# Sample values and sample outputs of a gated recurrence, carried through DRAM

## The chip, the cores and the metric

The kernel runs on one core of a Trainium2 chip. The metric is the device time of one execution in microseconds, the median of several runs. The engines are named as in the profile: PE (TensorE), DVE (VectorE), ACT (ScalarE), POOL (GpSimd), SP (SyncE, which here only issues DMAs).

## The reference

One inference step of two layers over 1024 prompt tokens and 8 sample tokens (one new token in each of 8 sequences), width 1024, all in fp32. The first layer is a gated linear recurrence (HGRN2) with 8 heads of 128 keys and 128 values, the second a sliding-window attention. The change touches only the first layer, and in it only the 8 sample tokens. For a head, cut to what matters:

```python
u = rmsnorm(h, norm_g) @ w_in
q, f, i, g = split(u)
q = silu(q);  k = (1 - lb) * sigmoid(-f);  v = i          # decay f_t = sigmoid(f) + lb * sigmoid(-f)
# prompt: chunkwise over 1024 tokens; sample: one step from the state s0 of each sequence b
S[b] = diag(decay[b]) @ s0[b] + outer(k[b], v[b])         # 128 keys x 128 values, an output
o[b] = S[b].T @ q[b]                                      # 128 values
o = rmsnorm(o, gnorm) * silu(g);  h = h + o @ w_out
```

So each head needs, for each of the 8 sequences b, an outer product of keys and values that is added to a decayed 128x128 state, and a product of that state with the query. In the program's layout the features lie on the partitions and the tokens along the row: a tile of T = 1032 columns holds 1024 prompt tokens and then the 8 sample tokens.

## The kernel before

**The loop.** The first layer's projection is a loop of HEADS + 1 = 9 turns `it`, each with 9 slots. In turn `it` the slots compute the projections of head `it` (three weight blocks of 128 columns, f, q and v; a block takes three `unit`s of 344 token columns, 24 matmuls each, L1569), while the recurrence of head r = it - 1 runs between the units on PE, and at slot 0 the output of head p = it - 2. Turn 8 has the first gate blocks in its units, and the sums for the heads' norms. The output of head 7 follows behind the loop (L1705), then two units, then its norm sums `head_sums(7)` (L1708).

**Slot 8 and slot 0.** At slot 8 PE does `value_broadcast(r)` (L1625) and `chunk_sums(r)` (L1631). The sample state keeps keys on partitions and (sequence, value) along the row, so the update needs each sequence's values on all 128 partitions. POOL's `decode_parts` (L649) multiplies the sample columns of RAWV with the identity into VD (128 x 1024) in slot 4; PE multiplies VD with a matrix of ones, which puts the values on every partition in two PSUM banks, VB0 and VB1; DVE's `decode_state` (L1142) multiplies these with the keys into VK, `decode_add` (L1151) adds VK to the decayed state SS, and `chunk_states` (L1157) makes the eight prompt states ST. DVE does these behind the evacuation of slot 8's unit. At slot 0 of the next turn PE does a unit, then `head_output` (L1640): 8 chunks, each with VH x AT (L1647) and, from the second on, ST x QU (L1650), which waits for its step of ST; then the sample outputs OS (L1655), 8 matmuls with SS of a sequence as the 128x128 stationary operand and one query column moving, which write 8 columns. Behind it comes `diagonal` of head r (L1596), 32 matmuls on four quarters of 32 columns of the array. It waits for `q1_done`, which DVE's `first_query` (L1109) signals; that waits for the group O1, the second half of the head output, as it overwrites QU.

**Banks.** The recurrence's PSUM groups (`turn_groups`, L54) take five banks in turn; a group waits until the one five before it is read. ACT's `copy_head` (L811) copies O0, O1 and OS into A, the sample columns of A from the 8 columns of OS. ACT's `square_head` (L817) squares all 1032 columns of A of a head for its norm sums.

**Queues.** Each engine runs its instructions in the written order and waits for semaphores. All DMAs are issued by SP (L451 on). In a turn SP issues three weight loads (each waits until POOL has made the low part of the block three before, `lo_value`), `states(it - 1)` (SS from DRAM, waits for the OS of the head before) and `store_states(it - 1)`. A weight load fills one of three buffers; its block is prepared by ACT (L751) once the block three before is done on PE. A matmul of the recurrence (plain fp32) is two instructions in the profile, one of the units (fp32r) is one.

Of the kernel before, what the change touches and what calls it, by code (L numbers as in the profile page):

```python
# [21 lines left out]
P = 128  # L22
KT = D // P
SEQ, DEC = 1024, 8
# [29 lines left out]
def turn_groups(it):  # L54

    slots = [[] for _ in range(9)]
    tail, rec = it - 2, it - 1
    if 0 <= tail < HEADS:
        slots[0] += [("O0", tail, "act"), ("O1", tail, "act"), ("OS", tail, "act")]
    if 0 <= rec < HEADS:  # L60
        slots[0] += [(f"D{i}", rec, "dve") for i in range(NC // 2)]
        for s in range(1, NL):
            slots[s].append((f"L{s}", rec, "dve"))
        slots[2] += [("VT0", rec, "act"), ("VT1", rec, "act")]
        slots[7] += [("T0", rec, "act"), ("T1", rec, "act")]
        slots[8] += [("VB0", rec, "prod"), ("VB1", rec, "prod"), ("S0", rec, "state"), ("S1", rec, "state")]
    if it == HEADS:
        for m in range(HEADS - 1):
            slots[m + 1] += [(f"N{i}", m, "act") for i in range(NU)]
    if it == HEADS + 1:  # L70
        slots[2] += [(f"N{i}", HEADS - 1, "act") for i in range(NU)]
    return [g for s in slots for g in s]
# [55 lines left out]
def build(nc, ctx, ins, outs):  # L128
# [3 lines left out]
    x_d, w_d, gain_d, lbl_d, st_d, lmask_d, imask_d, ident_d, cs_d, amask_d, smask_d, sink_d, sinks_d, kc_d, vc_d = ins  # L132
    y_d, stp_d, sts_d, kwin_d, vwin_d = outs
    h1_d = nc.dram_tensor("h1_spill", [P, KT, T], fp32, kind="Internal").ap()
    sg_d = nc.dram_tensor("gate_spill", [P, HP, T], fp32, kind="Internal").ap()


# [81 lines left out]
    PSN = sb("PSN", [DEC, P], fp32, rk)  # L219

    rp = [max(ra[0], rb_[0])]
    amask = sb("amask", [P, 2 * P], fp32, rp)
    sink = sb("sink", [P, 16], fp32, rp)
    smask = sb("smask", [P, DEC], fp32, rp)
# [15 lines left out]
    def sem(name):  # L240
        return ctx.enter_context(nc.semaphore(name))
# [29 lines left out]
    upd_k = sem("upd_k")  # L271
    fp_step = sem("fp_step")
    fp_done = sem("fp_done")
    vd_done = sem("vd_done")
    ss_in = sem("ss_in")
    ss_decayed = sem("ss_decayed")
    ss_prod = sem("ss_prod")
# [1 line left out]
    st_step = sem("st_step")  # L279
    stp_out = sem("stp_out")  # L280
    sts_out = sem("sts_out")
    sqn_done = sem("sqn_done")
    rn_done = sem("rn_done")
    norm_done = sem("norm_done")
# [96 lines left out]
    def half(i):  # L381
        return slice(i * 512, (i + 1) * 512)
# [4 lines left out]
    def read_value(r, name):  # L387
        who = GROUPS[GINDEX[name, r]][2]
        if who == "state":
            return st_step, NC * r + 4 * (int(name[1]) + 1)  # L390
        if who == "prod":
            return ss_prod, 2 * r + int(name[2]) + 1
        return (read_act if who == "act" else read_dve), READ_COUNT[name, r]

    def bank(r, name):
        return R[GINDEX[name, r] % NBANK_R]
# [55 lines left out]
    def _(sp):  # L452
# [32 lines left out]
        states(0)  # L485
        load_weights(3)
        load_weights(4)
        for it in range(HEADS + 1):
            load_weights(3 * it + 5)
            if it >= 2:  # L490
                states(it - 1)
            load_weights(3 * it + 6)
            load_weights(3 * it + 7)
            if it >= 1:
                store_states(it - 1)

        for n in range(N_AO, N_AO + 3):
            load_weights(n)

# [7 lines left out]
        first_residual(1)  # L507
        sp.wait_ge(stp_out, 16 * HEADS)
        sp.wait_ge(sts_out, 16 * HEADS)
        for t, d in ((amask, amask_d), (sink, sink_d), (smask, smask_d), (sinks, sinks_d), (CS, cs_d)):  # L510
            sp.dma_start(t[:], d).then_inc(const2_in, 16)
        for m in range(KT):
# [93 lines left out]
    def _(pool):  # L606
# [40 lines left out]
                                    ).then_inc(upd_k, 1)  # L647

        def decode_parts(r):  # L649
            pool.wait_ge(unit_read, 9 * r + 9)  # L650
            if r:
                pool.wait_ge(ss_prod, 2 * r)
            nc.gpsimd.tensor_tensor(VD[:, 0:SEQ].rearrange("p (b e) -> p b e", b=DEC),
                                    ident[:].unsqueeze(1).broadcast_to([P, DEC, P]),
                                    RAWV[:, SEQ:T].unsqueeze(2).broadcast_to([P, DEC, P]), ALU.mult).then_inc(vd_done, 1)
            pool.wait_ge(ss_in, 16 * (r + 1))
            pool.wait_ge(fp_done, r + 1)
            nc.gpsimd.tensor_tensor(SS[:], SS[:], DECC[:, r % 2, NC:].unsqueeze(2).broadcast_to([P, DEC, P]), ALU.mult
                                    ).then_inc(ss_decayed, 1)
# [82 lines left out]
    def _(act):  # L742
# [66 lines left out]
                nc.scalar.activation(dst[:, half(i)], bank(r, f"{name}{i}")[:], ACT.Copy).then_inc(read_act, 1)  # L809

        def copy_head(p):  # L811
            for name, cols in (("O0", half(0)), ("O1", half(1)), ("OS", slice(SEQ, T))):
                act.wait_ge(group_done, group_value(p, name))
                nc.scalar.activation(A[:, p, cols], bank(p, name)[:, 0:cols.stop - cols.start], ACT.Copy
                                     ).then_inc(read_act, 1)

        def square_head(m):  # L817
            if m == 0:
                act.wait_ge(ss_prod, 2 * (HEADS - 1))
            else:  # L820
                act.wait_ge(group_done, group_value(m - 1, "N2"))
            act.wait_ge(read_act, READ_COUNT["OS", m])
            nc.scalar.activation(SQN[:], A[:, m, :], ACT.Square).then_inc(sqn_done, 1)

        def norm_head(m):
# [240 lines left out]
    def _(dve):  # L1066
# [74 lines left out]

        def decode_state(r):  # L1142
            for i in range(2):
                dve.wait_ge(group_done, group_value(r, f"VB{i}"))
                dve.wait_ge(k_done, r + 1)
                nc.vector.tensor_tensor(VK[:, half(i)].rearrange("p (b e) -> p b e", b=4),
                                        bank(r, f"VB{i}")[:].rearrange("p (b e) -> p b e", b=4),
                                        K[r % 2][:, SEQ + 4 * i:SEQ + 4 * i + 4].unsqueeze(2).broadcast_to([P, 4, P]),
                                        ALU.mult).then_inc(ss_prod, 1)

# [61 lines left out]
        for it in range(HEADS + 1):  # L1212
            r = it - 1
            for slot in range(9):
                j, i = divmod(slot, 3)
                if slot == 0 and it:
                    dve.wait_ge(k_done, it)
                if slot == 3 and it:
                    dve.wait_ge(q_done, it)
                if slot == 6 and it:  # L1220
                    dve.wait_ge(group_done, group_value(it - 1, "VT1"))
                if slot == 8 and it:
                    dve.wait_ge(vd_done, it)
                evacuate(9 * it + slot, i, (RAWF, RAWQ, RAWV)[j])
                if r >= 0:
                    if slot == 0:
                        first_query(r)
                        for c in range(NC // 2):
                            merge_diagonal(r, c)
                    if 0 < slot < NL:  # L1230
                        update_q(r, slot)
                        merge_level(r, slot)
                    if slot == 8:
                        decode_state(r)
                        decode_add(r)
                        chunk_states(r)
                if slot == 7 and it < HEADS:
                    apply_query_gate(it)
                if it == HEADS and slot >= 2:
                    apply_norm(slot - 2)  # L1240
# [306 lines left out]
    def _(pe):  # L1547
# [74 lines left out]
                                           by_blocks(QU[:, first:first + w], l)[:, :, 1, :], start=True, stop=True)  # L1622
            ins.then_inc(group_done, 1)

        def value_broadcast(r):  # L1625
            pe.wait_ge(vd_done, r + 1)
            for i in range(2):
                b = open_group(r, f"VB{i}")
                nc.tensor.matmul(b[:], ones[:], VD[:, half(i)], start=True, stop=True).then_inc(group_done, 1)  # L1629

        def chunk_sums(r):  # L1631
            for i in range(2):
                pe.wait_ge(*read_value(r, f"T{i}"))
# [6 lines left out]
        def head_output(r):  # L1640
            pe.wait_ge(*read_value(r, f"L{NL - 1}"))
            pe.wait_ge(upd_q, NL * r + NL)
            for i in range(2):
                b = open_group(r, f"O{i}")
                for c in range(4 * i, 4 * i + 4):
                    cols = b[:, (c % 4) * P:(c % 4 + 1) * P]
                    ins = nc.tensor.matmul(cols, VH[:, c, :], AT[:, c, :], start=True, stop=(c == 0))  # L1647
                    if c:
                        pe.wait_ge(st_step, NC * r + c)
                        ins = nc.tensor.matmul(cols, ST[:, c - 1, :], QU[:, c * P:(c + 1) * P], start=False, stop=True)  # L1650
                ins.then_inc(group_done, 1)
            pe.wait_ge(ss_done, r + 1)
            b = open_group(r, "OS")
            for n in range(DEC):
                ins = nc.tensor.matmul(b[:, n:n + 1], SS[:, n, :], QDEC[:, r % 2, n:n + 1], start=True, stop=True)  # L1655
            ins.then_inc(group_done, 1)

        def head_sums(m):
# [20 lines left out]
        for it in range(HEADS + 1):  # L1679
            p, r = it - 2, it - 1  # L1680
            for slot in range(9):
# [4 lines left out]
                if r >= 0:  # L1686
# [10 lines left out]
                        for i in range(2):  # L1697
                            transposed(r, f"T{i}", K[r % 2], i)
                    if slot == 8:
                        value_broadcast(r)  # L1700
                        chunk_sums(r)
                if it == HEADS and 1 <= slot < HEADS:
                    head_sums(slot - 1)
# [253 lines left out]
```

## Time and profile before

| | |
|---|---|
| median of 3 runs | 1076.44 us (1076.37 to 1076.47) |
| the profiled execution | 1076.68 us, its span 1074.9 us |
| PE, DVE, POOL, ACT busy | 1033.7, 619.2, 436.0, 385.1 us |
| a steady turn of the loop (160.78 to 211.44) | 50.66 us |
| the last turn (414.15 to 477.08) | 62.93 us |

Line numbers are those of the kernel before. Busy times of PE overlap, as matmuls are pipelined: what an instruction costs is the distance between its start and that of the next one. In a timeline row the numbers are its start and its length in microseconds, x16 means that 16 instructions are merged, and what stands in brackets is the idle time of the engine before it and who ended it. PEld is the loading of the stationary operand.

### The profile page before, as it was taken

How to read it: one execution, taken by the hardware profiler on the slowest of the kernel's cores; microseconds unless marked ns; L12 is line 12 of the kernel's file. 1: busy time of each engine (PE TensorE's matmuls, PEld its weight loads, DVE VectorE, ACT ScalarE, POOL GpSimd, SP SyncE). 2: the span in 40 equal slices, each digit the busy share in tenths (PEclk: the TensorE clock that was granted, in tenths of full speed). 3: DMA queues.
4: the chain of work that ended last, by engine and by line, in shares of the span. 5: the costliest groups of instructions: out<-in, count | busy, mean ns of one | idle time of the engine just before them, and what ended most of it. 6: DMA issues, size and time to landing. Idle time of an engine off the chain costs nothing.

```text
span 1074.9 us, 22442 instructions
## 1 busy us (share of the span) xinstructions
PE 1033.7 (96%) x9392; PEld 964.5 (90%) x9392; DVE 619.2 (58%) x1195; ACT 385.1 (36%) x775; POOL 436.0 (41%) x294
## 2 busy tenths in 40 slices
PE   6999999999999999999999999999989999898996
PEld 5899999999999999899999999999988888677895
DVE  8153645554555546454843235357777878987835
ACT  4412212121213132645333233501037757654523
POOL 1245554645546463521225441343445333322243
PEclk9999999999999999999999999999989989999998
DMA  7111112021111202011314323211112113322103
GB/s 281 40 41 41 65 39 83 21 82 41 63 62 41 82 26 78 22 40 43 124 60 166 130 79 136 80 46 53 47 45 67 60 60 100 89 71 60 48 33 125
DMA packets 39812, 77.10 MB, mean 72 GB/s; under 512 B 5792, under 2 KB 24736, under 8 KB 39584
## 3 DMA queue, kind: packets, MB, share of 16 engines
q1 hardware_dynamic: 39712, 75.67, 21.2%
q8 instruction: 74, 1.21, 0.5%
q14 instruction: 26, 0.21, 0.1%
HBM read 58.12 MB, written 17.54 MB: 70 GB/s over the span
## 4 chain that ended last, share of the span: by engine, by line
PE 77%; DVE 12%; ACT 6%; issue 3%; POOL 1%; DMA 0%; DVEq 0%; SPq 0%; ACTq 0%; POOLq 0%
PE G L1566 54%; PE G L1821 4%; DVE SP L1403 4%; ACT SP L983 3%; PE R L1619 3%; DVE QNL L1388 3%; PE R L1669 1%; PE R L1593 1%; PE R L1636 1%; PE R L1647 1%; DVE PT L1421 1%; PE R L1629 1%; PE R L1655 1%; PE R L1662 1%; PE R L1650 1%
## 5 line engine op out<-in xcount | busy, mean ns | idle before, releaser
L1566 PE MATMUL G<-XH,WH 128*128 128x344 f32 x1176 | 387.3, 329 | 1.9 <-DVE RAWF L1079 1.9
L1566 PE MATMUL G<-XL,WH 128*128 128x344 f32 x1176 | 379.4, 323 | 2.3 <-DVE KE L1373 1.9
L1566 PE MATMUL G<-XH,WL 128*128 128x344 f32 x744 | 238.3, 320 | 0.0
L1566 PEld LDWEIGHTS G<-XH,WH 128*128 128x128 f32 x1176 | 223.0, 190 | 5.8 <-issue 2.2
L1566 PEld LDWEIGHTS G<-XL,WH 128*128 128x128 f32 x1176 | 222.9, 190 | 5.1 <-DVE WL L1069 2.2
L615 POOL TENSOR_TENSOR WL<-WR,WH 128x1024 fp32r<-128x1024 f32 x40 | 102.1, 2553 | 181.8 <-ACT WH L760 181.8
L760 ACT ACTIVATE WH<-WR 128x1024 fp32r<-128x1024 f32 x58 | 61.1, 1055 | 263.1 <-PE G L1566 167.1
L1566 PEld LDWEIGHTS G<-XH,WL 128*128 128x128 f32 x744 | 140.4, 189 | 0.0
L1566 PE MATMUL G<-XL,WL 128*128 128x344 f32 x432 | 139.7, 323 | 0.0
L646 POOL TENSOR_TENSOR K<-K,FP 128x512 f32<-128x512 f32 x48 | 77.6, 1617 | 90.5 <-PE R L1619 90.5
L698 POOL TENSOR_TENSOR SP<-SP,small 128x1024 f32<-128x1024 f32 (+1 forms) x32 | 57.3, 1790 | 136.0 <-DVE small L1414 136.0
L983 ACT ACTIVATE SP<-SP,small 128x256 f32<-128x256 f32 (+1 forms) x128 | 61.8, 484 | 68.4 <-DVE small L1403 68.4
L1566 PEld LDWEIGHTS G<-XL,WL 128*128 128x128 f32 x432 | 82.5, 191 | 0.4
L1079 DVE TENSOR_TENSOR RAWQ<-G,RB 128x344 f32<-128x344 f32 x27 | 14.0, 517 | 82.4 <-PE G L1566 82.4
L1566 PE MATMUL G<-GR,WL 128*128 128x344 f32 x192 | 61.4, 320 | 0.0
L1566 PE MATMUL G<-GR,WH 128*128 128x344 f32 x192 | 61.4, 320 | 0.0
L1566 PE MATMUL G<-AR,WH 128*128 128x344 f32 x192 | 61.3, 319 | 0.0
L1079 DVE TENSOR_TENSOR RAWV<-G,RB 128x344 f32<-128x344 f32 x27 | 14.0, 517 | 73.1 <-PE G L1566 73.1
L1403 DVE CUSTOM_DVE_ANT_0 SP<-R,amask,sink 128x256 f32<-128x256 f32 (+1 forms) x128 | 51.9, 458 | 1.5 <-PE R L1767 1.5
L1821 PE MATMUL G<-XL,WH 128*128 128x344 f32 x144 | 47.9, 333 | 0.5 <-DVE AR L1523 0.5
L714 POOL TENSOR_TENSOR KE<-KE,CS 128x1032 f32<-128x1032 f32 x8 | 27.2, 3395 | 49.5 <-DVE KE L1377 49.5
L1821 PE MATMUL G<-XL,WL 128*128 128x344 f32 x144 | 46.0, 319 | 0.0
(253 smaller groups left out, 1978.2 us busy)
## 6 DMA issues: line engine op xcount, KB each, us to landing
WR<-w SPq DMA_DIRECT2D x58, 512.0 KB, 3.6
A<-x SPq DMA_DIRECT2D x8, 516.0 KB, 8.3
RESO<-x SPq DMA_DIRECT2D x8, 516.0 KB, 4.7
h_spill<-H SPq DMA_DIRECT2D x8, 516.0 KB, 2.9
gate_spill<-EV SPq DMA_DIRECT2D x24, 172.0 KB, 1.9
RES<-h_spill SPq DMA_DIRECT2D x24, 172.0 KB, 3.0
y<-H SPq DMA_DIRECT2D x24, 172.0 KB, 1.9
SS<-states SPq DMA_DIRECT2D x8, 512.0 KB, 3.6
```

What stands on the lines that cost most here:

```text
L615: nc.gpsimd.tensor_tensor(WL[:, n % 3], WR[:, n % 3], WH[:, n % 3].bitcast(fp32), ALU.subtract).then_inc(lo_pool, 1)
L646: nc.gpsimd.tensor_tensor(low, low, decay(l, 1).unsqueeze(2).broadcast_to([P, SEQ // (2 * h), h]), ALU.mult).then_inc(upd_k, 1)
L698: nc.gpsimd.tensor_tensor(sp_, sp_, small[:, q % 2, 4, :].unsqueeze(2).broadcast_to([P, 4, keys.stop - keys.start]), ALU.mult).then_inc(p_ ...
L714: nc.gpsimd.tensor_tensor(KE[:], KE[:], CS[:, 0], ALU.mult).then_inc(q_cos, 1)
L760: nc.scalar.activation(WH[:, n % 3], WR[:, n % 3], ACT.Copy).then_inc(hi_done, 1)
L983: nc.scalar.activation(SP_[q % 2][:, i, keys], SP_[q % 2][:, i, keys], ACT.Exp, bias=sm[:, 0, i:i + 1], scale=-1.0, accum_out=sm[:, 2, i:i ...
L1079: nc.vector.tensor_tensor(dst[:, seg(i)], G[i][:, 0:TU], RB[:, seg(i)], ALU.mult).then_inc(unit_read, 1)
L1388: nc.vector.scalar_tensor_tensor(QNL[:, q % 2], pair(A, q), -1.0, QNH[:, q % 2].bitcast(fp32), ALU.mult, ALU.subtract).then_inc(qn_done, 1)
L1403: ins = nc.vector.tensor_tensor_reduce(out=SP_[q % 2][:, i, keys], in0=ps[:, keys], in1=amask[:, keys], scale=1.0, scalar=sink[:, h + i:h ...
L1566: return nc.tensor.matmul(G[unit_bank(NU * n + i)][:, 0:TU], w[:, n % 3, k, :], x[:, seg(i)], start=(k == 0 and p == 0), stop=(k == KT - 1 ...
L1619: ins = nc.tensor.matmul(b[v * w:v * w + w - h, first // 2:(first + w) // 2].rearrange("p (n h) -> p n h", h=h), K[r % 2][:, first:first + ...
L1821: return nc.tensor.matmul(G[unit_bank(u)][:, 0:TU], wt[:, k, :], x, start=(w == 0), stop=(w == 11))
```

## The change

1. The broadcast of the sample values is done by DMA. A new step `sample_values(r)` on SP stores the 8 sample columns of RAWV to DRAM (128 rows of 32 bytes), waits for it, and loads the 1024 numbers back as one row that is repeated on all 128 partitions of VD. POOL's product with the identity, PE's `value_broadcast` and the groups VB0 and VB1 are gone; DVE reads VD from SBUF, with a step of 8 elements, as the row is ordered value by value.
2. The sample outputs have the operands the other way round: the query column, repeated 32 times, is stationary, the 128 columns of SS move, and sequence n writes 32 equal rows of the quarter n % 4 of the array, in columns 0 to 127 or 128 to 255. ACT copies 128 x 256 into OSR. A new step `sample_outputs(p)` on SP stores one row of each quarter to DRAM, waits for it, and loads it turned, 8 numbers for each of 128 partitions from places 512 bytes apart, into the sample columns of A. `square_head` waits for that load.

```diff
-        slots[8] += [("VB0", rec, "prod"), ("VB1", rec, "prod"), ("S0", rec, "state"), ("S1", rec, "state")]
+        slots[8] += [("S0", rec, "state"), ("S1", rec, "state")]
...
+        def sample_values(r):
+
+            sp.wait_ge(unit_read, 9 * r + 9)
+            sp.dma_start(vs_d[r], RAWV[:, SEQ:T]).then_inc(vs_out, 16)
+            if r:
+                sp.wait_ge(ss_prod, 2 * r)
+            sp.wait_ge(vs_out, 16 * (r + 1))
+            sp.dma_start(VD[:, 0:SEQ], vs_d[r].rearrange("e b -> (e b)").unsqueeze(0).broadcast_to([P, SEQ])
+                         ).then_inc(vd_in, 16)
+
+        def sample_outputs(p):
+
+            sp.wait_ge(read_act, READ_COUNT["OS", p])
+            sp.dma_start(os_d[p].rearrange("(j v) e -> v j e", v=4), OSR[0:P:32, :].rearrange("v (j e) -> v j e", j=2)
+                         ).then_inc(os_out, 16)
+            sp.wait_ge(os_out, 16 * (p + 1))
+            sp.dma_start(A[:, p, SEQ:T], os_d[p].rearrange("n e -> e n"), allow_slow_non_contiguous=True).then_inc(os_in, 16)
+
         for it in range(HEADS + 1):
             load_weights(3 * it + 5)
+            if it >= 1:
+                sample_values(it - 1)
             if it >= 2:
                 states(it - 1)
             load_weights(3 * it + 6)
+            if it >= 2:
+                sample_outputs(it - 2)
             load_weights(3 * it + 7)
             if it >= 1:
                 store_states(it - 1)
 
+        sample_outputs(HEADS - 1)
         for n in range(N_AO, N_AO + 3):
             load_weights(n)
...
         def decode_parts(r):
-            pool.wait_ge(unit_read, 9 * r + 9)
-            if r:
-                pool.wait_ge(ss_prod, 2 * r)
-            nc.gpsimd.tensor_tensor(VD[:, 0:SEQ].rearrange("p (b e) -> p b e", b=DEC),
-                                    ident[:].unsqueeze(1).broadcast_to([P, DEC, P]),
-                                    RAWV[:, SEQ:T].unsqueeze(2).broadcast_to([P, DEC, P]), ALU.mult).then_inc(vd_done, 1)
...
+            act.wait_ge(group_done, group_value(p, "OS"))
+            if p:
+                act.wait_ge(os_out, 16 * p)
+            nc.scalar.activation(OSR[:], bank(p, "OS")[:, 0:2 * P], ACT.Copy).then_inc(read_act, 1)
...
             act.wait_ge(read_act, READ_COUNT["OS", m])
+            act.wait_ge(os_in, 16 * (m + 1))
             nc.scalar.activation(SQN[:], A[:, m, :], ACT.Square).then_inc(sqn_done, 1)
...
-                dve.wait_ge(group_done, group_value(r, f"VB{i}"))
+                dve.wait_ge(vd_in, 16 * (r + 1))
                 dve.wait_ge(k_done, r + 1)
                 nc.vector.tensor_tensor(VK[:, half(i)].rearrange("p (b e) -> p b e", b=4),
-                                        bank(r, f"VB{i}")[:].rearrange("p (b e) -> p b e", b=4),
+                                        VD[:, 0:SEQ].rearrange("p (e b) -> p b e", b=DEC)[:, 4 * i:4 * i + 4],
...
-                    dve.wait_ge(vd_done, it)
+                    dve.wait_ge(vs_out, 16 * it)
...
-        def value_broadcast(r):
-            pe.wait_ge(vd_done, r + 1)
-            for i in range(2):
-                b = open_group(r, f"VB{i}")
-                nc.tensor.matmul(b[:], ones[:], VD[:, half(i)], start=True, stop=True).then_inc(group_done, 1)
...
             for n in range(DEC):
-                ins = nc.tensor.matmul(b[:, n:n + 1], SS[:, n, :], QDEC[:, r % 2, n:n + 1], start=True, stop=True)
+                j, v = divmod(n, 4)
+                ins = nc.tensor.matmul(b[32 * v:32 * v + 32, j * P:(j + 1) * P],
+                                       QDEC[:, r % 2, n:n + 1].broadcast_to([P, 32]), SS[:, n, :], start=True, stop=True)
```

SP also waits for the last store of sample outputs before it loads the attention's masks, which share OSR's place.

## Rows read from the trace of the kernel before

**Rows 1.** Page, part 1: busy us (share of the span), instructions.
```profile
PE 1033.7 (96%) x9392; PEld 964.5 (90%) x9392; DVE 619.2 (58%) x1195; ACT 385.1 (36%) x775; POOL 436.0 (41%) x294
```

**Rows 2.** Waits of PE, longest first: in total, times, longest us.
```profile
PE R L1767 <- DVE small L1403: 10.2, 13, 1.2
```

**Rows 3.** Windows, a steady turn and the last: busy us, PEclk, DMA, GB/s.
```profile
160.78:211.44 50.66, 50.66 (x669) 48.10 (x667) 26.71 (x46) 12.08 (x16) 26.11 (x21) 1.00 0.17 55
...
414.15:477.08 62.93, 62.88 (x710) 56.09 (x709) 33.07 (x50) 30.84 (x45) 29.16 (x21) 1.00 0.13 44
```

**Rows 4.** Timeline of PE, slot 8 of the last turn.
```profile
473.42 1.88 PE L1629 MATMUL R<-VD,ones 128*128 128x512 f32 x4
475.13 1.95 PE L1636 MATMUL R<-VH,KTT 128*128 128x128 f32 x16
476.84 0.40 PE L1566 MATMUL G<-XH,WH 128*128 128x344 f32 x1
```

**Rows 5.** Timeline, from slot 8 of a turn into the next: DVE, POOL, PE.
```profile
106.69 0.52 DVE L1079 TENSOR_TENSOR RAWV<-G,RB 128x344 f32<-128x344 f32 x1 [3.00 <-PE G L1566]
...
107.48 0.69 DVE L1146 TENSOR_TENSOR VK<-R,K 128x512 f32<-128x512 f32 x1 [0.27 <-PE R L1629]
...
107.82 2.35 POOL L615 TENSOR_TENSOR WL<-WR,WH 128x1024 fp32r<-128x1024 f32 x1 [8.21 <-ACT WH L760]
...
109.07 2.18 DVE L1154 TENSOR_TENSOR SS<-SS,VK 128x1024 f32<-128x1024 f32 x1
...
111.49 2.72 DVE L1169 SCALAR_TENSOR_TENSOR ST<-ST,DECC,R 128x128 f32<-128x128 f32 x7
...
114.15 0.39 PE L1650 MATMUL R<-QU,ST 128*128 128x128 f32 x2
```

**Rows 6.** Groups of DVE by shape: count, busy us, mean ns, idle before.
```profile
L1154 DVE TENSOR_TENSOR SS<-SS,VK 128x1024 f32<-128x1024 f32 x8 | 17.5, 2185 | 0.3
...
L1139 DVE TENSOR_TENSOR QM<-QM,RAWQ 128x1024 f32<-128x1024 f32 x8 | 9.8, 1219 | 0.0
...
L1119 DVE TENSOR_TENSOR QU<-QM,FG 128x512 f32<-128x512 f32 x8 | 5.9, 739 | 0.0
```

**Rows 7.** Timeline, end of the head output and the diagonal behind it.
```profile
117.05 1.84 PE L1655 MATMUL R<-QDEC,SS 128*128 128x1 f32 x16
117.25 0.60 ACT L814 ACTIVATE A<-R 128x512 f32<-128x512 f32 x1 [1.19 <-PE R L1650]
117.35 0.69 DVE L1117 TENSOR_TENSOR QM<-QM,FG 128x512 f32<-128x512 f32 x1 [2.72 <-PE R L1650]
...
118.83 0.89 PE L1605 MATMUL R<-QM,K 128*32 128x48 f32 x64
...
119.64 0.43 PE L1566 MATMUL G<-XH,WH 128*128 128x344 f32 x1
```

**Rows 8.** Timeline of the first turn, where PE waits for QM.
```profile
67.21 0.86 DVE L1117 TENSOR_TENSOR QM<-QM,FG 128x512 f32<-128x512 f32 x1
...
68.17 0.89 PE L1605 MATMUL R<-QM,K 128*32 128x48 f32 x64 [1.50 <-issue]
```

**Rows 9.** Timeline of PE and ACT behind the last head's output.
```profile
485.75 0.41 PE L1566 MATMUL G<-XH,WH 128*128 128x344 f32 x1
...
486.20 1.07 ACT L823 ACTIVATE K<-A 128x1032 f32<-128x1032 f32 x1
...
493.39 1.90 PE L1662 MATMUL R<-K,ones 128*128 128x344 f32 x6
```

**Rows 10.** Waits of SP's queue: in total, times, longest us.
```profile
SPq L456 <- POOL WL L615: 330.0, 25, 29.9
```

**Rows 11.** DMA issues: count, KB each, median us to landing.
```profile
SS<-states SPq DMA_DIRECT2D x8, 512.0 KB, 3.6
...
stp<-ST SPq DMA_DIRECT2D x8, 64.0 KB, 1.6
...
SGD<-gate_spill SPq DMA_DIRECT2D x2, 16.0 KB, 2.4
```

More of the change, by code:

```diff
@@ L134, in build @@
     h1_d = nc.dram_tensor("h1_spill", [P, KT, T], fp32, kind="Internal").ap()
+    vs_d = nc.dram_tensor("sample_values", [HEADS, P, DEC], fp32, kind="Internal").ap()
+    os_d = nc.dram_tensor("sample_outputs", [HEADS, DEC, P], fp32, kind="Internal").ap()
     sg_d = nc.dram_tensor("gate_spill", [P, HP, T], fp32, kind="Internal").ap()
@@ L221, in build @@
     rp = [max(ra[0], rb_[0])]
+    OSR = sb("OSR", [P, 2 * P], fp32, [rp[0]])
     amask = sb("amask", [P, 2 * P], fp32, rp)
@@ L273, in build @@
     fp_done = sem("fp_done")
-    vd_done = sem("vd_done")
+    vs_out = sem("vs_out")
+    vd_in = sem("vd_in")
     ss_in = sem("ss_in")
@@ L281, in build @@
     sts_out = sem("sts_out")
+    os_out = sem("os_out")
+    os_in = sem("os_in")
     sqn_done = sem("sqn_done")
@@ L390, in read_value @@
             return st_step, NC * r + 4 * (int(name[1]) + 1)
-        if who == "prod":
-            return ss_prod, 2 * r + int(name[2]) + 1
         return (read_act if who == "act" else read_dve), READ_COUNT[name, r]
@@ L509, in _ @@
         sp.wait_ge(sts_out, 16 * HEADS)
+        sp.wait_ge(os_out, 16 * HEADS)
         for t, d in ((amask, amask_d), (sink, sink_d), (smask, smask_d), (sinks, sinks_d), (CS, cs_d)):
@@ L811, in copy_head @@
         def copy_head(p):
-            for name, cols in (("O0", half(0)), ("O1", half(1)), ("OS", slice(SEQ, T))):
+            for name, cols in (("O0", half(0)), ("O1", half(1))):
                 act.wait_ge(group_done, group_value(p, name))
-                nc.scalar.activation(A[:, p, cols], bank(p, name)[:, 0:cols.stop - cols.start], ACT.Copy
-                                     ).then_inc(read_act, 1)
+                nc.scalar.activation(A[:, p, cols], bank(p, name)[:], ACT.Copy).then_inc(read_act, 1)
+            act.wait_ge(group_done, group_value(p, "OS"))
+            if p:
+                act.wait_ge(os_out, 16 * p)
+            nc.scalar.activation(OSR[:], bank(p, "OS")[:, 0:2 * P], ACT.Copy).then_inc(read_act, 1)
         def square_head(m):
@@ L1699, in _ @@
                     if slot == 8:
-                        value_broadcast(r)
                         chunk_sums(r)
```

## Prediction, written before the change was timed

> **What bounds the kernel now.** I read the busy shares first. PE is busy 96% of the span, the next engine 58% [rows 1], so the time is PE's instruction stream unless the change opens a wait in it. The waits of PE come second: the longest sum in the list is 10.2 us, and it stands in the attention, far behind the change [rows 2]. The windows come third. One steady turn of the loop lasts 50.66 us, and PE is busy for all 50.66 at a granted clock of 1.00 (the 2.4 GHz level), DVE for 26.7, POOL for 26.1, DMA at 0.17; the last turn is 62.93, PE 62.88 [rows 3]. So in the eight turns that the change touches PE alone sets the pace, and each PE instruction removed is worth its full distance to the next one, until another engine's result comes late. The last view is the timeline around the two edited places, read for start-to-start distances, because busy times of matmuls overlap.
>
> **Part 1: the value broadcast leaves PE.** L1629 starts at 473.42, the chunk sums behind it at 475.13, the next unit at 476.84 [rows 4]. The four instructions of the broadcast take 1.71 us, 0.427 each, and the sixteen of the chunk sums behind them another 1.71, 0.107 each. Neither has a start-up cost beside it, so none stays behind. 8 heads x 1.71 = 13.7 us off.
>
> What does it uncover? DVE's chain in the same slot. Before: evacuation ends 107.21, VK starts at 107.48 (both halves wait for PE), SS add from 109.07, then eight steps of ST, the last seven from 111.49; PE needs the first ST at 114.15 [rows 5]. It has it at 111.49, 2.7 us early. After the change PE gets there 1.71 us sooner, at 112.44; DVE starts VK at 107.2, as vd_in is long there. What VK from SBUF costs isn't in the trace. Below: 0.69 each, the PSUM form [rows 5]; L1119 with three strided SBUF operands is near it (0.74) [rows 6]. Above: in this very stretch POOL works in SBUF and the SS add takes 2.185 for 1024 columns, where L1139 takes 1.219 [rows 6], so 1.09 for 512. I take 0.69 for the first (POOL starts at 107.82) and 1.09 for the second: SS add at 109.0, as now, first ST at 111.5, 0.9 us to spare. The later steps need no slack: ST comes every 0.35 (2.72/7), PE asks every four matmuls, 0.44 at the step of part 2. So 0 here, and a stall only if the pair of VK takes over 2.7 us.
>
> POOL loses an instruction in slot 4. It is worth nothing: POOL is 26 of 50.7 busy [rows 3] and its level updates wait for PE.
>
> **Part 2: sample outputs in column quarters.** Now 16 instructions (two for each matmul) from 117.05 to 118.83, 1.78 us at 0.111 each, as the weight loads (128x128) pace them; the diagonal L1605 follows [rows 7]. After: 128 moving columns, 32 stationary. One behind the other such matmuls would go at the 0.107 of L1636, 1.71 [rows 4]: no gain. Four quarters at once is 0.43. L1605, which uses the same quarters, does 64 instructions of 48 columns in 0.81, 13 ns each [rows 7], against 40 ns if 48 columns took 48/128 of 0.107. It overlaps, so I take 0.45 to 0.65.
>
> But that gain can't be kept in full. The diagonal also waits for q1_done. DVE's QM can start only when the group O1 is done: 117.35, 0.30 after the OS matmuls start; it takes 0.69, to 118.04 [rows 7]. In the first turn, where PE does wait for it, QM ends at 68.07 and PE starts at 68.17 [rows 8]. So the diagonal can start at 118.14 at best, 1.09 after OS starts, and any OS time below 1.09 is idle. Worth 118.83 - 118.14 = 0.69 in the 7 turns in which a diagonal follows: 4.8 us. (ACT's copy of O1, which frees D3's bank, ends at 117.85 and is not later.) In the eighth a unit follows and nothing is waited for. There the saving is the 1.78 less 0.65, and less some 0.2 for the change of tile shape on the way in and out, which I put at what L1605 takes over 64 ideal steps (0.81 - 64 x 0.010): 0.9.
>
> **Part 3: the DMAs.** SP gets four more issues and two blocking waits a turn. Its queue can bear them: in 25 waits for POOL's WL it stands idle for 330 us, 13 us each [rows 10]. sample_values stands behind load 3it+5, at the start of the turn: a store of 4 KB (at most the 1.6 of stp), the wait, and VD (512 KB, 3.6 as SS [rows 11]) end within some 7 us, and DVE wants VD in slot 8, some 45 us later. Behind it stand the states, which wait for the OS of slot 0 and which POOL wants in slot 4. sample_outputs (2 to 3 us until SP is free) stands behind load 3it+6, which comes with slot 3, and ahead of load 3it+7, which waits for slot 6. After the loop it holds back the three loads of N_AO on by 4 to 6 us; ACT takes the first of them up two blocks of units (some 23 us) later. The DMA engines are at 0.17 [rows 3], so 0.5 MB a turn more is hidden, and without that cover it would be the 3.6 us a turn. ACT's copy of 128x256 instead of 128x8 is off the path.
>
> The last head alone is close. The chain behind its OS, from its start s: ACT copy of O1 from s+0.2 to s+0.8 (as it stands to OS in [rows 7]), copy of OS to s+1.2, SP, store landed s+2.9 (1.6), load landed s+3.0+X, square 1.07 [rows 9], so PE can start head_sums(7) at s+4.2+X. PE comes there after OS (0.65) and two units (485.75 to 493.39 [rows 9]: 7.64) at s+8.3. It stalls if X is over 4.1. X is the load turned by strides, 1024 pieces of 4 bytes, 64 for each of 16 engines. The gate load SGD moves 512 pieces of 32 bytes in 2.4 and stp 128 pieces in 1.6 [rows 11], so 24 more per engine cost 0.8, 33 ns each, and 56 more 1.9: X = 3.5. Ends: 2.4 (as SGD) and 4.8 (twice SGD). I take 3.5, no stall; the upper end stalls 0.7.
>
> The sum: 13.7 + 4.8 + 0.9 = 19.4. The profiled execution took 1076.68 (span 1074.9), 0.24 above the median of the runs, which is within what runs differ by: 1057.3 by its own time, 1076.44 - 19.4 = 1057.0 us as a median.
>
> **Rivals.**
> (a) DVE's VK is slow and ST comes late. For: VD is read with a step of 32 bytes, and no row has an SBUF operand with so wide a step; POOL shares the stretch. If a step doubles the time, VK is 1.4 + 1.8 = 3.2, and 3.6 if POOL weighs on both: 0.5 to 0.9 of stall in 8 heads, 4 to 7 us, so 1061 to 1064. Against: L1119 with steps of 8 bytes pays nothing. The Trainium skill, "SBUF — State Buffer", section "Door 1: The DMA port swizzle", says that consecutive accesses within one 16-byte line run at full bandwidth and each that crosses to a new line pays; by that rule the 8-byte steps are free, as the trace has them, and the 32-byte steps are not, which is this rival. Chance 0.27.
> (b) The quarters don't overlap (128 columns, not 48, and the same bank): OS stays 1.7, the 4.8 and the 0.9 are gone: 1062.7. Against: L1605. Chance 0.07.
> (c) The turned load is slower than 4.8: at 7 the stall is 2.9, 1060. Chance 0.12.
> (d) The same load goes so slowly that the kernel loses: it needs X of 4.1 + 19.4 = 23.5 us, 0.37 us for each of 64 pieces, eleven times the 33 ns above. At 30 us the stall is 25.9 and the kernel ends at 1076.44 - 19.4 + 25.9 = 1082.9. Nothing in the rows is near it. Chance 0.03. The Trainium skill, "VectorE: DVE Perf Modes", section "The three transpose paths", warns that a plain DMA that transposes by strides is 19 times slower than the hardware's own transposing DMA; taken as an estimate on the 1.6 us of stp this gives 30 us, so by that rule (d) is what happens; SGD's 512 short pieces in 2.4 speak against it, but they aren't single elements.
> (e) A queue effect hides the change: SP's new waits make weights late, as much as was gained, 1076. SP's idle 330 us speak against it. Chance 0.01.
>
> **The numbers.** The forecast has 0.50, (a) 0.27, (b) 0.07, (c) 0.12, (d) 0.03, (e) 0.01. Its own range is 1055.5 to 1058.5 (the OS of the last head, a unit's switching, a diagonal that starts 0.1 earlier or later in 7 turns). The range of 8 in 10 goes from 1055.2 to 1062.6: it takes in the nearer half of (a) and nearly all of (c) and leaves out the end of (a), (b), (d) and (e), 0.2 in all. Within 0.2% is 1074.3 to 1078.6, what a measurement of this kernel can't tell from no change. Faster 0.96 (the forecast, (a), (b) and (c)), same 0.01, slower 0.03.
>
> **What would show it.** A steady turn of 48.26 us (50.66 - 1.71 - 0.69). L1629 gone, and L1636 0.16 behind the unit. In the OS group 16 matmuls some 30 ns apart, then an idle time of PE of some 0.5 us ahead of L1605, ended by DVE's QM, in 7 turns: new in the list of PE's waits. No wait of L1650 for DVE's ST; if there is one, (a) holds, and VK's mean duration says why. No wait ahead of the last head_sums; if there is one, X is over 4.1, and the DMA table gives it. Wrong altogether would be a longer turn elsewhere, in slots 1 to 7, where nothing is touched but POOL and SP.

## The result, and the profile after

The changed kernel takes 1063.68 us (1063.2 to 1065.85, 4 runs), the kernel before 1076.4 (1073.99 to 1076.47); the ratio is 0.9889, with an interval of 0.9872 to 0.9906. It is faster by 12.7 us. The forecast was a gain of 19.4 and a range of 1055.2 to 1062.6; the time lies 1.1 us above the range.

The profiled execution has a span of 1061.4 us. Page, part 1, and the list of what PE waited for:

```profile
PE 1010.1 (95%) x9360; PEld 944.2 (89%) x9360; DVE 631.4 (59%) x1195; ACT 386.8 (36%) x775; POOL 428.8 (40%) x286
```

```profile
PE R L1788 <- DVE small L1429: 10.2, 13, 1.2
...
PE R L1670 <- DVE ST L1192: 6.9, 8, 1.0
PE R L1631 <- issue: 4.0, 8, 1.5
```

PE has 23.6 us less to do (1033.7 busy in [rows 1]), and its list has two new waits. The first, for ST, comes eight times. The second is that of the diagonal: 0.37 in each of seven turns; the 1.5 of the first turn was there before [rows 8]. A steady turn, as a window:

```profile
216.98:266.48 49.50, 48.19 (x663) 46.05 (x663) 28.31 (x46) 12.30 (x16) 25.28 (x19) 1.00 0.21 67
```

It is 49.50 us, against 50.66 in [rows 3] and the 48.26 forecast, and PE is now idle for 1.3 of it. The timeline of the two edited places shows where (DVE, POOL and PE; slot 8's unit has just ended):

```profile
255.07 4.23 DVE L1172 TENSOR_TENSOR VK<-VD,K 128x512 f32<-128x512 f32 x2
255.77 2.61 POOL L643 TENSOR_TENSOR WL<-WR,WH 128x1024 fp32r<-128x1024 f32 x1 [8.21 <-ACT WH L782]
...
258.33 1.82 POOL L663 TENSOR_TENSOR FP<-FG 128x512 f32<-128x512 f32 x1
...
259.34 1.89 DVE L1180 TENSOR_TENSOR SS<-SS,VK 128x1024 f32<-128x1024 f32 x1
...
261.15 0.28 DVE L1192 COPY ST<-R 128x128 f32<-128x128 f32 x1
261.46 2.72 DVE L1195 SCALAR_TENSOR_TENSOR ST<-ST,DECC,R 128x128 f32<-128x128 f32 x7
...
261.48 0.49 PE L1670 MATMUL R<-QU,ST 128*128 128x128 f32 x2 [0.94 <-DVE ST L1192]
...
261.81 0.39 PE L1667 MATMUL R<-AT,VH 128*128 128x128 f32 x2
...
264.58 0.64 PE L1676 MATMUL R<-SS,QDEC 128*32 128x128 f32 x16
...
264.79 0.70 DVE L1143 TENSOR_TENSOR QM<-QM,FG 128x512 f32<-128x512 f32 x1 [0.18 <-PE R L1670]
...
265.60 0.89 PE L1631 MATMUL R<-QM,K 128*32 128x48 f32 x64 [0.37 <-issue]
```

DVE starts VK right behind its evacuation, as forecast, but the pair takes 4.23 us instead of 1.78. The chain behind it is late: the first ST (the copy L1192) is done at 261.43, and L1670 (the old L1650), which could have gone at 260.38, starts at 261.48, 1.10 late. In [rows 5] the first ST was there 2.7 us before PE asked for it. The restart costs a little more: the next matmul, L1667, follows the pair that had waited after 0.33, where it follows after 0.22 in a turn without the wait. So a turn loses 1.21. The other place is as forecast: the 16 OS matmuls start at 264.58, QM at 264.79 behind O1, the diagonal at 265.60, 1.02 behind OS (1.09 forecast, 1.78 in [rows 7]).

The two VK instructions are not alike. The first row is the source line's, with the shortest, the median and the longest duration (the median of 16 that fall into two kinds), the second a piece of the chain of waits:

```profile
L1172 DVE TENSOR_TENSOR VK<-VD,K x16: 1081/2152/3231, 106.6 to 466.3; 128x512 f32<-128x512 f32 x16
```

```profile
256.08 3.23 DVE VK L1172
```

The first takes 1.08, the second 3.23. The DMAs, with count, KB and median us to landing, are:

```profile
SS<-states SPq DMA_DIRECT2D x8, 512.0 KB, 5.0
VD<-sample_values SPq DMA_DIRECT2D x8, 512.0 KB, 4.0
...
sample_values<-RAWV SPq DMA_DIRECT2D x8, 4.0 KB, 4.5
...
A<-sample_outputs SPq DMA_DIRECT2D x8, 4.0 KB, 2.3
```

The load that is turned by strides lands in 2.3 us (X, forecast 3.5), so nobody waits at the last head but ACT: ACT's square, which waits for it, starts at 479.37 and takes 1.07, and PE comes to the norm sums at 482.42, with no wait:

```profile
479.37 1.07 ACT L849 ACTIVATE K<-A 128x1032 f32<-128x1032 f32 x1 [4.09 <-DMA A<-sample_outputs]
```

```profile
482.42 1.03 PE L1684 MATMUL R<-K,ones 128*128 128x344 f32 x3
```

A last point on where the time went. In the chain of waits, the units of block 28, behind the last head's sums, start at 495.29 before and at 484.31 after, 10.98 us earlier. Of these, 0.51 were there before PE came to any edited instruction: the first turn's diagonal starts at 68.17 before and at 67.66 after, and between 67.11 and 68.52 in the other kernels below, whose edits also come later on PE. From that diagonal on, the part that was edited gave 10.47 us. The span fell by 13.5. The other 2.5 lie behind block 28, mostly in the second layer, which no edit touches, and where the granted clock differs between executions. Here are 90 us of units before and 89 after; PEclk is the third figure from the end:

```profile
700.00:790.00 90.00, 88.08 (x550) 87.83 (x549) 62.09 (x71) 8.49 (x8) 40.48 (x16) 0.98 0.15 50
```

```profile
689.00:778.00 89.00, 87.08 (x554) 86.82 (x553) 62.09 (x71) 8.49 (x8) 41.03 (x16) 1.00 0.15 50
```

The same 504 unit matmuls take 81.13 us in the one and 79.56 in the other. The runs of the kernel before spread from 1073.99 to 1076.47 by themselves. So I compare parts by the turn and by the start of block 28, and whole kernels by their medians.

### The profile page after: what moved, and what is told of

It is laid out like the page before. It is cut to its first block, busy times and chain, and to the rows that moved or that the text cites. A ratio compares the mean times of both kernels' runs of the same rounds, so it can differ in the third digit from the quotient of the medians.

```text
span 1061.4 us, 22401 instructions
## 1 busy us (share of the span) xinstructions
PE 1010.1 (95%) x9360; PEld 944.2 (89%) x9360; DVE 631.4 (59%) x1195; ACT 386.8 (36%) x775; POOL 428.8 (40%) x286
## 3 DMA queue, kind: packets, MB, share of 16 engines
q8 instruction: 74, 1.21, 0.5%
## 4 chain that ended last, share of the span: by engine, by line
PE 71%; DVE 15%; ACT 7%; issue 5%; POOL 1%; DMA 0%; DVEq 0%; SPq 0%; ACTq 0%; POOLq 0%
PE G L1592 51%; PE G L1842 5%; DVE SP L1429 4%; ACT SP L1009 4%; PE R L1645 3%; DVE VK L1172 3%; DVE QNL L1414 3%; PE R L1691 2%; PE R L1619 1%; PE R L1684 1%; PE R L1670 1%; DVE PT L1447 1%; PE R L1667 1%; PE G L1696 1%; PE R L1631 1%
## 5 line engine op out<-in xcount | busy, mean ns | idle before, releaser
L643 POOL TENSOR_TENSOR WL<-WR,WH 128x1024 fp32r<-128x1024 f32 x40 | 104.3, 2608 | 178.8 <-ACT WH L782 178.8
```

What stands on the lines that cost most here:

```text
L643: nc.gpsimd.tensor_tensor(WL[:, n % 3], WR[:, n % 3], WH[:, n % 3].bitcast(fp32), ALU.subtract).then_inc(lo_pool, 1)
```

## The experiments

Beside the change, eight kernels were run. A steady turn is the distance between the starts of the chunk sums of two turns in the profiled execution, given for one pair of turns (other pairs of the same kernel differ by up to 0.1); "block 28" is the start of its units in the profiled execution. The interval of each ratio is that of 95%.

| kernel | steady turn | block 28 | median us | ratio to before (interval) |
|---|---|---|---|---|
| before | 50.68 | 495.29 | 1076.4 | |
| the change | 49.48 | 484.31 | 1063.68 | 0.9889 (0.9872 to 0.9906) |
| e4: values only | 50.16 | 490.06 | 1069.9 | 0.9951 (0.9934 to 0.9969) |
| e3: outputs only | 50.00 | 488.84 | 1067.45 | 0.9932 (0.9912 to 0.9951) |
| e1: no step, store turned | 48.9 to 52.9 | 490.75 | 1069.13 | 0.994 (0.992 to 0.996) |
| e2: VK in slot 7 | 48.28 | 475.18 | 1055.24 | 0.9815 (0.9797 to 0.9832) |
| e10: WL behind SS | 48.28 | 475.64 | 1056.59 | 0.9824 (0.9803 to 0.9846) |
| e9: WL in halves | 48.65 | 478.66 | 1058.49 | 0.984 (0.9813 to 0.9868) |
| e8: e2 and QM first | 47.72 | 470.68 | 1051.01 | 0.9775 (0.9754 to 0.9797) |
| e12: e2 and an extra store | irregular | 512.72 | 1090.53 | 1.0138 (1.0091 to 1.0186) |

The kernel before ran beside each group, with medians of 1074.48 for the first four and 1076.52 for the others; the ratios are to those runs.

**The two parts alone.** e3, the changed kernel with POOL's product, PE's broadcast and the groups VB0 and VB1 back and without `sample_values`:

```diff
-                                        VD[:, 0:SEQ].rearrange("p (e b) -> p b e", b=DEC)[:, 4 * i:4 * i + 4],
+                                        bank(r, f"VB{i}")[:].rearrange("p (b e) -> p b e", b=4),
...
+                        value_broadcast(r)
                         chunk_sums(r)
```

> Only the second part of the change: sample outputs in column quarters and turned through DRAM; the values' broadcast stays on POOL and PE. Theory (the diagonal waits for QM, the parts are independent): turn 50.67 - 0.67 = 50.0, the last head 0.9 less, together 5.6: 1070.8. Rival (the gain of the quarters comes out in full): turn 49.5, 9.5 in all, 1066.9.

Measured: turn 49.96 to 50.01 (the chunk sums of two turns stand below), block 28 earlier by 6.45, 1067.45 us. The turn is the one forecast: QM behind O1 holds back the rest of the quarters' gain.

```profile
257.51 1.95 PE L1656 MATMUL R<-VH,KTT 128*128 128x128 f32 x16
```

```profile
307.47 1.95 PE L1656 MATMUL R<-VH,KTT 128*128 128x128 f32 x16
```

e4, the changed kernel with the old OS matmuls and copy back and without `sample_outputs`:

```diff
-                ins = nc.tensor.matmul(b[32 * v:32 * v + 32, j * P:(j + 1) * P],
-                                       QDEC[:, r % 2, n:n + 1].broadcast_to([P, 32]), SS[:, n, :], start=True, stop=True)
+                ins = nc.tensor.matmul(b[:, n:n + 1], SS[:, n, :], QDEC[:, r % 2, n:n + 1], start=True, stop=True)
```

> Only the first part of the change: values spread by DMA; sample outputs as before, one moving column with SS stationary. Theory: the broadcast's 1.71 less, ST's lateness of some 1.1 more: turn 50.1, 8 heads give 5.5 us: 1070.9. Rival (the ST wait has to do with the new outputs, not with VK): turn 48.96, 13.7 in all, 1062.7.

Measured: turn 50.16, block 28 earlier by 5.23, 1069.9 us, and the same wait:

```profile
PE R L1650 <- DVE ST L1172: 6.9, 8, 1.0
```

6.9 us in 8 times, as with both parts. The lateness of ST belongs to the values alone, and takes back most of the broadcast's 1.71. The two parts add up: counted from the first turn's diagonal, e3 gives 5.83, e4 4.77, together 10.60 against 10.47.

**The step alone.** e1 changes the order of the row, so that VD needs no step:

```diff
-            sp.dma_start(vs_d[r], RAWV[:, SEQ:T])
+            sp.dma_start(vs_d[r].rearrange("b e -> e b"), RAWV[:, SEQ:T], allow_slow_non_contiguous=True)
...
-                                        VD[:, 0:SEQ].rearrange("p (e b) -> p b e", b=DEC)[:, 4 * i:4 * i + 4],
+                                        VD[:, half(i)].rearrange("p (b e) -> p b e", b=4),
```

> The changed kernel, but the sample values are stored to DRAM sequence by sequence (turned by the store, 1024 pieces of 4 bytes), so that DVE reads VD without a step. Still in slot 8, beside POOL. Theory (the step of 32 bytes doubles the time, and POOL's work doubles it again: 2 x 2 x 0.53 = 2.12): VK falls from 2.15 to 1.0 to 1.1 us each, the pair from 4.24 to about 2.1, PE's wait for the first ST (6.9 us in the list) goes, a steady turn falls from 49.48 to 48.3, the kernel by 8 to 1055.5. Rival 1 (POOL alone makes it slow, the step is free): VK stays at 2.1, turn 49.5, time unchanged. Rival 2 (the turned store is slow and vd_in comes late): a wait of DVE ahead of VK appears.

Measured: 1069.13, slower than the change. The wait for ST is gone, and DVE's groups by shape (mean ns behind the comma) say that VK takes 0.68, less than the 1.0 to 1.1 expected:

```profile
L1180 DVE TENSOR_TENSOR SS<-SS,VK 128x1024 f32<-128x1024 f32 x8 | 26.4, 3298 | 0.3
...
L1172 DVE TENSOR_TENSOR VK<-VD,K 128x512 f32<-128x512 f32 x16 | 10.3, 683 | 0.0
```

Timeline of the same place in e1:

```profile
257.32 1.28 DVE L1172 TENSOR_TENSOR VK<-VD,K 128x512 f32<-128x512 f32 x2
258.01 2.84 POOL L643 TENSOR_TENSOR WL<-WR,WH 128x1024 fp32r<-128x1024 f32 x1 [8.21 <-ACT WH L782]
...
258.64 3.30 DVE L1180 TENSOR_TENSOR SS<-SS,VK 128x1024 f32<-128x1024 f32 x1
```

Now both VK are through before POOL's WL has got going, and it is SS that stands, 3.30 us instead of 1.2. So all three expectations missed in part: the step costs less than double, and POOL doesn't double anything, it stops something. The loss came from elsewhere. SP's timeline shows that from the issue of the turned store to the next step behind SP's wait for it 10.7 us pass (this includes its place in the queue behind a weight load; in the change the same wait is over 4.3 us after the issue), and PE's timeline shows two of the stops that appear:

```profile
266.25 0.78 SPq L495 DMA_DIRECT2D sample_values<-RAWV  x1
276.94 0.32 SPq L499 DMA_DIRECT2D VD<-sample_values  x1
```

```profile
277.12 0.72 PE L1645 MATMUL R<-QU,K 128*28 128x16 f32 x44 [0.70 <-issue]
```

```profile
285.00 0.29 PE L1645 MATMUL R<-QU,K 128*24 128x16 f32 x14 [1.86 <-issue]
```

PE stands in the middle of a group of matmuls with nothing to wait for that the profile shows, 9.5 us in all, in some turns and not in others. The stops begin 5.5 to 17 us after the store is issued; the second one shown begins 6 us after it had landed. In the two longest turns (52.9 and 52.4) the mean granted clock is 0.97 besides.

**VK moved.** e2 keeps the step, and moves `decode_state` from the head of slot 8's chain to the end of slot 7:

```diff
                     if slot == 8:
-                        decode_state(r)
                         decode_add(r)
                         chunk_states(r)
...
                 if it == HEADS and slot >= 2:
                     apply_norm(slot - 2)
+                if slot == 7 and r >= 0:
+                    decode_state(r)
```

> The changed kernel with the step kept, but the two VK instructions are moved from slot 8 to the end of slot 7, where POOL has nothing to do. Theory (step x2 and POOL x2): VK 1.1 to 1.2 us each. The step alone: 2.15 as before. POOL alone: 0.6 to 0.7. In all three the chain of slot 8 is shorter by the pair, so the wait for ST goes: turn 48.3, time 1055.5, if the slowness of VK in the chain is what cost the 8 us. If something else delays ST (bank, S0, DECC), the wait stays.

Measured: 1055.24, turn 48.28, no wait for ST; block 28 is 20.1 earlier than before, where the forecast of the change had 19.4. DVE's groups by shape, and the timeline of slot 8:

```profile
L1172 DVE TENSOR_TENSOR VK<-VD,K 128x512 f32<-128x512 f32 x16 | 17.9, 1164 | 0.0
...
L1180 DVE TENSOR_TENSOR SS<-SS,VK 128x1024 f32<-128x1024 f32 x8 | 9.7, 1215 | 0.0
```

```profile
251.41 1.22 DVE L1180 TENSOR_TENSOR SS<-SS,VK 128x1024 f32<-128x1024 f32 x1
252.11 2.79 POOL L643 TENSOR_TENSOR WL<-WR,WH 128x1024 fp32r<-128x1024 f32 x1 [8.22 <-ACT WH L782]
...
254.86 1.04 POOL L663 TENSOR_TENSOR FP<-FG 128x512 f32<-128x512 f32 x1
```

With the step and without POOL, VK takes 1.16, without the step 0.68, so the step makes it 1.7 times as long. SS, which starts before POOL, takes 1.22, and WL, which starts 0.70 into it, 2.79 instead of the 2.35 of [rows 5]. The difference, 0.44, is about the 0.52 that SS still had to run.

**POOL moved, and cut.** e10 makes POOL wait for SS before the WL of slot 0; e9 cuts that WL in two.

```diff
+                if slot == 0 and it >= 2:
+                    pool.wait_ge(ss_done, it - 1)
```
```diff
+            for i in range(2):
+                ks = slice(HK * i, HK * i + HK)
+                ins = nc.gpsimd.tensor_tensor(WL[:, n % 3, ks], WR[:, n % 3, ks], WH[:, n % 3, ks].bitcast(fp32),
+                                              ALU.subtract)
+            ins.then_inc(lo_pool, 1)
```

> The changed kernel, VK in slot 8 with its step, but POOL waits for DVE's SS add before its WL of slot 0. Theory (no overlap): VK 1.1 each, SS 1.22, first ST some 2.4 us earlier, no wait of PE for ST, turn 48.3, time 1055.5. If the step alone made VK slow (2.1 each whatever POOL does): VK pair 4.2, ST wait about as now (0.3 to 0.9), turn 49.2 or more.

```profile
251.23 2.17 DVE L1174 TENSOR_TENSOR VK<-VD,K 128x512 f32<-128x512 f32 x2
...
253.44 1.23 DVE L1182 TENSOR_TENSOR SS<-SS,VK 128x1024 f32<-128x1024 f32 x1
...
254.74 2.38 POOL L643 TENSOR_TENSOR WL<-WR,WH 128x1024 fp32r<-128x1024 f32 x1 [11.03 <-DVE SS L1182]
...
256.54 0.39 PE L1672 MATMUL R<-QU,ST 128*128 128x128 f32 x2
```

VK is at the same place as in the change, with the same step, and the pair takes 2.17. Only POOL has moved. The turn is 48.28, with no wait for ST. The last head is a control within the same run: the WL beside its VK comes behind the loop and isn't held back, and there the pair takes 4.24 again and PE waits 0.3 for ST.

```profile
456.65 4.24 DVE L1174 TENSOR_TENSOR VK<-VD,K 128x512 f32<-128x512 f32 x2
457.35 2.60 POOL L643 TENSOR_TENSOR WL<-WR,WH 128x1024 fp32r<-128x1024 f32 x1 [11.69 <-ACT WH L784]
```

So the stall takes both: the step with POOL out of the way costs nothing (e10), and POOL without the step costs nothing either (e1 has no wait for ST).

> The changed kernel, VK in slot 8 with its step, but POOL's WL of slot 0 is made in two halves of 512 columns. Theory (a two-operand SBUF instruction of DVE and one of POOL do not overlap at all: the second VK, which starts just behind POOL's WL, stands until WL ends): the second VK falls from 3.23 to about 2.1 us, as it waits for the first half alone; the second half then holds up SS; ST comes 0.3 to 0.4 earlier, turn 49.1. Rival (both run side by side, each at half its rate): VK's two times and the turn of 49.48 don't change.

```profile
252.85 3.15 DVE L1182 TENSOR_TENSOR VK<-VD,K 128x512 f32<-128x512 f32 x2
253.55 3.55 POOL L650 TENSOR_TENSOR WL<-WR,WH 128x512 fp32r<-128x512 f32 x2 [8.21 <-ACT WH L792]
...
256.04 2.14 DVE L1190 TENSOR_TENSOR SS<-SS,VK 128x1024 f32<-128x1024 f32 x1
...
258.42 2.71 DVE L1205 SCALAR_TENSOR_TENSOR ST<-ST,DECC,R 128x128 f32<-128x128 f32 x7
...
258.43 0.49 PE L1680 MATMUL R<-QU,ST 128*128 128x128 f32 x2
```

The pair falls from 4.23 to 3.15, so the second VK from 3.2 to 2.1, and the two halves of WL together (3.55) are 0.9 longer than WL was in the change (2.61), close to one VK: they take turns. The rival (side by side at half rate) would have changed nothing; and at half rate the second VK would take 2.3 at most (twice 1.16), not 3.23. The turn came out better than expected, 48.65 against 49.1; PE is idle for ST for 0.1 in it.

**What held the diagonal.** e8 is e2 with the wait for O1 behind the first product:

```diff
-            if r:
-                dve.wait_ge(group_done, group_value(r - 1, "O1"))
             odd = QM[:, :, 32:48]
             gates = FG[:, 0:SEQ].rearrange("p (c n two) -> p c n two", n=16, two=2)
             nc.vector.tensor_tensor(odd, QM[:, :, 1:32:2], gates[:, :, :, 1], ALU.mult).then_inc(q1_done, 1)
             qu = QU[:].rearrange("p (c n two) -> p c n two", n=16, two=2)
+            if r:
+                dve.wait_ge(group_done, group_value(r - 1, "O1"))
```

> The kernel with VK in slot 7 (turn 48.28), and DVE's first product of first_query (QM) ahead of its wait for the group O1, which only QU needs. Theory (what keeps part of the quarters' gain from coming out is QM behind O1): the idle time of PE ahead of the diagonal (0.37 in each turn) goes, turn 47.9, the kernel some 2.6 us below the kernel with VK in slot 7, 1052.6. Rival (a floor of its own in the switch from the OS matmuls to the diagonal, such as a drain or the bank D3 waiting for ACT's copy of O1): the 0.37 stays, turn 48.28.

```profile
257.50 0.64 PE L1677 MATMUL R<-SS,QDEC 128*32 128x128 f32 x16
...
257.96 0.86 PE L1632 MATMUL R<-QM,K 128*32 128x48 f32 x64
```

Measured: the diagonal starts 0.46 behind OS, without a wait. The turn is 47.72, which is 0.56 shorter than in e2 where I had expected the 0.37 of idle time, and the kernel takes 1051.01 us, 25.5 below the kernel before and 12.7 below the change by the medians. The quarters do overlap: 16 instructions of 128 columns take 0.46, 29 ns each, against 107 one behind the other.

**The turned store.** e12 is e2 with one more DMA, which nothing on SP waits for (DVE waits for it 40 us later, when it overwrites the source):

```diff
+            sp.dma_start(xs_d[r].rearrange("b e -> e b"), RAWV[:, SEQ:T], allow_slow_non_contiguous=True).then_inc(xs_out, 16)
             sp.wait_ge(vs_out, 16 * (r + 1))
```

> The kernel with VK in slot 7 (turn 48.28), and in each turn one more DMA that nobody on SP waits for: the 8 sample columns stored turned, 1024 pieces of 4 bytes, to a place that nothing reads. Theory for the kernel with the turned store (the pieces keep the DMA engines busy for some 10 us, and PE's instructions come late through them): PE stands still in the middle of groups of matmuls, released by nothing, in irregular turns, 1 to 4 us in a turn, some 6 to 8 us in all. Rival (it was SP's blocking wait, which moved the loads): no such stops, turn 48.3 in every turn.

```profile
PE R L1650 <- issue: 20.9, 12, 4.4
```

```profile
225.00:235.00 10.00, 8.97 (x160) 7.97 (x158) 5.76 (x11) 0.62 (x1) 2.88 (x2) 1.00 0.19 23
235.00:245.00 10.00, 5.62 (x50) 5.48 (x41) 1.30 (x2) 4.14 (x6) 4.00 (x2) 0.66 0.24 85
```

Measured: 1090.53, slower than the kernel before; PE stands for 20.9 us in the recurrence's level matmuls (L1650) and 2.6 in units, released by nothing that the profile shows. That is three to four times the 6 to 8 us that I had expected. Of the windows, 10 us each, the first begins 3.3 us after one of these stores was issued: the DMA engines are shown 19% busy and move 23 GB/s, and PE's longest stop, 4.4 us, lies in the second window. In that one the mean granted clock is 0.66, so it was at its lower level for part of it after PE had stood; over the whole loop the mean is 0.97, against 1.00 in e2. Block 28 starts 37.5 us later than in e2: 23.5 are the stops, and PE is busy for 13.5 us more (424.4 against 410.9 from 60 us to block 28), for the same matmuls at a lower clock. That the turned store causes the stops is shown, with no wait of SP in between. How it does so is not shown, as the profile names no releaser. That PE's instructions come late through the DMA engines would fit (the page lists two queues of the kind "instruction"), but no run tests it.

## Why the prediction was wrong

The step that failed is in part 1, "I take 0.69 for the first (POOL starts at 107.82) and 1.09 for the second", and the "So 0 here" that follows from it. The pair took 4.23 where the sum had 1.78, well over the 2.7 us at which the prediction itself saw a stall begin. The stall came in all eight heads: L1670 started 1.10 late in seven and 0.45 late in the last (against where the matmuls ahead would have let it), and the restart cost 0.11 each time, together 9.0 us. With it the sum is 19.4 - 9.0 = 10.4, and from the first turn's diagonal on the edited part gave 10.47.

Two things were wrong in that term. The smaller one is that a step of 32 bytes isn't free: VK takes 1.08 to 1.16 and not 0.68. That was rival (a), with the rule of the Trainium skill beside it ("SBUF — State Buffer", section "Door 1: The DMA port swizzle"). By that rule a step past the 16-byte line pays, and the runs agree, with a factor of 1.7. But with POOL elsewhere it would have cost nothing (e10). The larger one is that I read the SS row as a rate ("1.09 for 512"), DVE at half speed beside POOL. The rows said something else, had I laid them on the time axis. In [rows 5] POOL's WL ends at 110.17, 1.10 after SS starts, and SS takes 2.18, 1.22 of it its own: it had stood until WL was through. With a rate the loss grows with the instruction's own length, with a stop it hangs on who starts first. The first VK, longer by its step, ends after WL has been issued, and the second waits for the whole rest of it. So rival (a) named the right wait, with a price that was too low: 4 to 7 us for a pair of 3.2 to 3.6, where the pair was 4.23 and the loss 9.0. It was too low even by the prediction's own rate, since a doubled second VK would be 2 x 1.09 = 2.2 and not 1.8. The range, which held only the nearer half of (a), missed. That 1063.68 lies inside the rival's 1061 to 1064 is partly luck: 0.5 us before the first diagonal and 2.5 behind block 28 fell to the changed kernel in stretches that no edit touches. The wait had a chance of 0.27; it should have had the larger one.

Point by point, the rest:
- The broadcast is worth 1.71 in each head: right. e2 and e10, where the chain is out of the way, have turns of 48.28 (forecast 48.26), and e2 gives 19.58 from the first diagonal to block 28 (forecast 19.4).
- QM behind O1 caps the gain of the quarters at 0.69 a turn: right, 0.68 in e3, and e8 shows that QM was what held it.
- The quarters overlap, rival (b) falls: 0.46 for the OS group. For the last head 1.70 became 0.64 (474.18 to the unit at 474.82), a gain of 1.1 where I had 0.9. The 0.2 put aside there for the change of tile shape fits: from OS to a unit it is 0.64, from OS to the diagonal 0.46 (e8).
- X was 2.3, at my lower end of 2.4 and not 3.5; rivals (c) and (d) fall. The Trainium skill ("VectorE: DVE Perf Modes", section "The three transpose paths") gives its factor of 19 only for a large innermost stride at the destination, a condition that the prediction left out. This load writes 8 numbers side by side in each partition and has its large stride at the source, so neither the rule nor the 30 us that I estimated from it applied. The runs have no transposing DMA, so the factor itself was not measured. The store of e1 has its large stride at the destination; it was slow (10.7 us to the end of SP's wait), and it was not in the change.
- Rival (e): in a steady turn SP issued the load of the states 5.2 us after the first weight load instead of 3.9, and the first load behind the loop some 3 us later than before, and no engine's list of waits has a new wait for them. SS landed in 5.0 instead of 3.6; its load is issued 0.4 behind that of VD. The small store of the values took 4.5, not 1.6; it is issued 0.5 behind a weight load. SP waited 30 us for it in all, at no cost.

Open are where the first turn's 0.5 us and more between executions come from, and how the turned store stops PE.

## What to carry to other kernels

When DVE instructions with two SBUF operands stand beside POOL instructions as these do, don't give them a rate: lay both on the time axis and let one wait for the end of the other. Who is issued first decides, and a small lengthening of one instruction can put it behind a long one. When work leaves the bounding engine, its place was cover for the chains beside it; count their slack with the new order of starts, and if it is near zero, move what can be done earlier (VK in slot 7, QM ahead of its wait) together with the change: here that doubles the gain, 25.5 us instead of 12.7. If data must be turned on the way through DRAM, try it on the load first: here the turned load cost nothing, and the turned store more than the step that it saved.

## What the runs showed of the hardware

- DVE's tensor_tensor with two SBUF operands and POOL's tensor_tensor exclude each other in every pair looked at here. VK takes 1.08 to 1.16 alone, 3.23 when POOL's WL is ahead of it, about 2.1 with WL in halves. SS takes 1.22 alone and 1.89 to 3.30 beside POOL. It holds the other way: POOL's first FP product takes 1.04 in e2, and 2.02 before, beside SS. With one operand in PSUM DVE isn't stopped: the second VK of the kernel before ran in 0.69 in the middle of WL.
- A product of 512 columns with one operand read at a step of 32 bytes takes DVE 1.08 to 1.16 us instead of 0.68.
- A 4 KB load in 1024 pieces of 4 bytes lands in 2.3 us. A 4 KB store in as many pieces, behind a weight load, keeps SP waiting for 10.7 (e1), and from 5.5 us after its issue on PE stops in mid-group (9.5 us in all in e1, 23.5 in e12), though the DMA engines are shown 19% busy in a window ahead of such a stop.
- Matmul instructions with 32 stationary columns, dealt over the four quarters, went at 29 ns each for 128 moving columns of fp32 (e8).
- A PE that had waited 0.94 for ST took 0.33 to the next pair of matmuls instead of 0.22.
